# Dilated attention in a decoder trunk: whole causal score rows before, near blocks and the keys of the query's class modulo 4 after

## The reference

```python
DIL_PATTERNS = ((128, 1), (512, 4), (2048, 16))
def dilated_prompt(q, k, v):
    outs, lses = [], []
    for w, d in DIL_PATTERNS:       # the rows of each class modulo d, apart
        o, lse = band_attn(sub(q), sub(k), sub(v), w // d)   # 0 <= t - j <= w // d
        ...
    return combine_branches(outs, lses)
```

## Time and profile before

| | |
|---|---|
| runs | 2828.29, 2823.35, 2825.64 us; median 2825.64 |
| profiled execution | 2823.23 us, its span 2821.4 |
| TensorE, share of the span | 99% |
| DVE, POOL, ACT | 62%, 51%, 33% |
| granted TensorE clock, mean | 0.999 |
| dilated attention with its linear units, first score to the end of the last pair | 1460 to 1727 us of the span |

### The profile page before, as it was taken

How to read it: one execution, slowest core, us unless ns; L and a number is a source line. 1 busy time by engine, 2 the same in 40 slices (tenths; PEclk the granted TensorE clock), 3 DMA queues, 4 the chain that set the end, 5 groups by cost and what they waited for, 6 DMA issues and landing times. The chain is left out here.

```text
span 2821.4 us, 61139 instructions
## 1 busy us (share of the span) xinstructions
PE 2795.2 (99%) x22743; PEld 2661.7 (94%) x22743; DVE 1739.8 (62%) x3258; ACT 931.0 (33%) x2089; POOL 1450.0 (51%) x1178
## 2 busy tenths in 40 slices
PE   9999999999999999999999999999999999999998
PEld 8888999999999999999987778999999999999998
DVE  5555642248766676977953346523468666668877
ACT  4333422133322222433324445212324222224433
POOL 3222343332677777877431112433334777777775
PEclk9999999999999999999999999999999999999999
DMA  4111133421223232642222222234312232326432
GB/s 138 38 30 38 60 113 130 153 85 37 90 105 119 75 119 105 233 143 82 65 76 84 84 76 69 86 133 148 120 46 76 83 111 105 119 76 231 128 128 76
DMA packets 79799, 283.05 MB, mean 100 GB/s; under 512 B 10959, under 2 KB 16975, under 8 KB 70665
## 3 DMA queue, kind: packets, MB, share of 16 engines
q10 hardware_dynamic: 41581, 148.18, 14.7%
q1 hardware_dynamic: 38051, 132.55, 13.9%
HBM read 223.45 MB, written 57.49 MB: 100 GB/s over the span
## 5 line engine op out<-in xcount | busy, mean ns | idle before, releaser
L681 POOL TENSOR_SCALAR w_hi<-w_raw 128x512 fp32r<-128x512 f32 x236 | 153.1, 667 | 989.6 <-PE linear L830 779.3
L685 POOL TENSOR_TENSOR w_lo<-w_raw,w_hi 128x512 fp32r<-128x512 f32 x420 | 590.9, 1419 | 98.0 <-ACT w_hi L1654 82.6
L830 PE MATMUL linear<-h_hi,w_hi 128*128 128x344 f32 x1134 | 373.7, 330 | 1.2 <-issue 0.5
L830 PE MATMUL linear<-h_hi,w_lo 128*128 128x344 f32 x1134 | 362.2, 319 | 0.0
L830 PE MATMUL linear<-h_lo,w_hi 128*128 128x344 f32 x1134 | 362.2, 319 | 0.0
L685 POOL TENSOR_TENSOR w_lo<-w_sum,w_hi 128x512 fp32r<-128x512 f32 x186 | 268.8, 1445 | 147.1 <-ACT w_hi L1654 146.5
L1218 PE MATMUL ps_scores<-c,w_hi 128*128 128x258 f32 x1512 | 288.5, 283 | 0.0
L1218 PE MATMUL linear<-c,w_hi 128*128 128x258 f32 x1344 | 247.3, 284 | 1.3 <-POOL w_lo L685 1.3
L830 PE MATMUL linear<-g_hi,w_hi 128*128 128x344 f32 x744 | 240.2, 323 | 0.0
L830 PE MATMUL linear<-g_hi,w_lo 128*128 128x344 f32 x744 | 237.7, 320 | 0.0
L830 PE MATMUL linear<-g_lo,w_hi 128*128 128x344 f32 x744 | 237.4, 319 | 0.0
(11 more groups left out here) (478 smaller groups left out, 7302.1 us busy)
## 6 DMA issues: line engine op xcount, KB each, us to landing
w_raw<-in_w SPq DMA_DIRECT2D x214, 512.0 KB, 3.7
hid_spill<-hid_out ACTq DMA_DIRECT2D x22, 1032.0 KB, 4.4
t_spill<-hid_joined ACTq DMA_DIRECT2D x20, 1032.0 KB, 3.9
y_val<-t_spill ACTq DMA_DIRECT2D x40, 516.0 KB, 4.1
kv_slotc<-in_mem_cache_k ACTq DMA_DIRECT2D x8, 2048.0 KB, 8.5
kv_slotc<-in_mem_cache_v ACTq DMA_DIRECT2D x8, 2048.0 KB, 10.2
w_more<-in_w SPq DMA_DIRECT2D x32, 512.0 KB, 5.5
y_val<-hid_spill ACTq DMA_DIRECT2D x30, 516.0 KB, 3.9
```

The costliest lines, as they stand in the source:

```text
L681: pool.tensor_scalar(out, src, 1.0, 0.0, ALU.mult, ALU.add).then_inc(sem["hi_split"], 1)
L685: return pool.tensor_tensor(out, src, hi.bitcast(F32), ALU.subtract).then_inc(sem[event], 1)
L830: mm = pe.matmul(out, w[:, slot, cols], a, start=(k == 0 and j == 0), stop=(k == n - 1 and j == 2))
```

## The change

It takes the query blocks in rising order, one piece each. A piece holds the query's own and the preceding key block in full (near), and of all earlier blocks the keys of the query's class modulo 4 (far): 32 per block. Queries are taken by class: the 32 queries 4a + r are the weights of class r, and write the output partitions 32r to 32r + 31, once against far keys (every fourth, starting at r) and once against near keys. The far probabilities come first in a row, then the near. They are transposed by blocks of 128 columns; where the far width isn't a multiple of 128, the last block's surplus rows, which are near probabilities, are zeroed in ACT's copy by a factor from `rows1`. The far values have to lie by class: each pair's values go from `vnat1` to a DRAM scratch and back as `vfar1` (position 128 x class + feature, partition = key / 4). The near part of V is as before, the far part has a matmul per 128 far keys, class and head, with 32 columns. The mask is 448 wide and the same for all blocks.

```diff
-PIECES = [(qb, 4 * part, min(4, qb + 1 - 4 * part), part == 0, 4 * part + 4 > qb)
-          for qb in reversed(range(QB)) for part in range(1 + qb // 4)]
-SAMPLE_S = 8
+BLOCK_ORDER = (0, 1, 2, 3, 4, 5, 6, 7)
+CLASSES = 4
+FAR = P // CLASSES
+PIECES = [(qb, max(0, qb - 1), min(2, qb + 1), FAR * max(0, qb - 1)) for qb in BLOCK_ORDER]
+SAMPLE_S = 5
-HALVES = [2 if piece[2] > 2 else 1 for piece in PIECES] + [1]
+HALVES = [2 if piece[3] else 1 for piece in PIECES] + [1]
...
-LAST_FILL = [("S", 3), ("V", 0), ("T", 1), ("S", 4), ("V", 1), ("T", 2), ("S", 5), ("V", 2), ("T", 3), ("S", 6), ("V", 3), ("T", 4),
-             ("S", 7), ("V", 4), ("T", 5), ("S", "sample"), ("V", 5), ("T", 6), ("S", 8), ("V", 6), ("T", 7), ("S", 9), ("V", 7),
-             ("S", 10), ("T", 8), ("S", 11), ("V", 8), ("T", 9)]
+LAST_FILL = [("S", 3), ("V", 0), ("T", 1), ("S", 4), ("V", 1), ("T", 2), ("S", "sample"), ("V", 2), ("T", 3), ("S", 5), ("V", 3), ("T", 4),
+             ("S", 6), ("V", 4), ("T", 5), ("S", 7), ("V", 5), ("T", 6)]
+LAST_SPLITS = {3: (0,), 4: (1,), "sample": (2,), 5: (3, 4), 6: (5, 6), 7: (7, 8)}
+LAST_BEGINS = {"sample": (0,), 5: (1, 2), 6: (3, 4), 7: (5, 6)}
 DIL_WIDE = {1: [("S", 1)],
             2: [("S", 2), ("T", 0)],
-            3: [("S", 3), ("V", 0), ("T", 1)],
-            4: [("S", 4), ("V", 1), ("T", 2)],
...
-            11: [("S", 10), ("T", 8)],
-            12: [("S", 11), ("V", 8), ("T", 9)]}
+            4: [("S", 3), ("V", 0), ("T", 1)],
+            5: [("S", 4), ("V", 1), ("T", 2)],
+            7: [("S", "sample"), ("V", 2), ("T", 3)],
+            8: [("S", 5), ("V", 3), ("T", 4)],
+            10: [("S", 6), ("V", 4), ("T", 5)],
+            11: [("S", 7), ("V", 5), ("T", 6)]}
-DIL_DRAIN = {0: [("V", 9), ("T", 10)], 1: [("V", 10), ("T", 11)], 2: [("V", 11), ("T", "sample")], 3: [("V", "sample")],
-             4: [("R", "sample")]}
+DIL_DRAIN = {0: [("V", 6), ("T", 7)], 1: [("V", 7), ("T", "sample")], 2: [("V", "sample")], 3: [("R", "sample")]}
...
+        v_scratch = nc.dram_tensor("v_scratch", (SEQ, P), F32, kind="Internal").ap()
...
@@ TensorE, score @@
-                        for h in range(2):
-                            r = HEAD * h
-                            for c in range(0, P, 32):
-                                mm = pe.matmul(ps_s[c:c + 32, 512 * h:512 * h + P * nb],
-                                               q1_of[i][r:r + HEAD, P * qb + c:P * qb + c + 32],
-                                               keys1[i][r:r + HEAD, P * kb:P * kb + P * nb], start=True, stop=True)
+                        for of, start, end, step_ in (("far", 0, far * CLASSES, CLASSES), ("near", P * kb, P * kb + P * nb, 1)):
+                            for h in range(2):
+                                for r in range(CLASSES if end > start else 0):
+                                    rows, first = slice(HEAD * h, HEAD * h + HEAD), start + (r if of == "far" else 0)
+                                    to = 512 * h + (0 if of == "far" else far)
+                                    mm = pe.matmul(ps_s[FAR * r:FAR * r + FAR, to:to + (end - start) // step_],
+                                                   q1_of[i][rows, P * qb + r:P * qb + P:CLASSES], keys1[i][rows, first:end:step_],
+                                                   start=True, stop=True, skip_group_check=True)
...
@@ TensorE, mix (behind the near part) @@
+                    if far:
+                        pe.wait_ge(loads["vfar"], 16 * i + 16)
+                        pe.wait_ge(sem["turned_in"], at("turned_in", ph, 0, done + 2))
+                        for b in blocks_of(k, 1):
+                            for c in range(CLASSES):
+                                for h in range(2):
+                                    r, at_ = HEAD * h, place_in_half(h, 1, b) + FAR * c
+                                    mm = pe.matmul(ps_o[r:r + HEAD, FAR * c:FAR * c + FAR], vfar1[:, b, P * c + r:P * c + r + HEAD],
+                                                   pt1[:, at_:at_ + FAR], start=False, stop=(b == blocks_of(k, 1)[-1]),
+                                                   skip_group_check=True)
...
@@ ACT, exponential @@
-                    act.wait_ge(sem["biased"], at("biased", ph, 0, BIAS_ORDER.index(k if k == "sample" else closing(k)) + 1))
+                    act.wait_ge(sem["biased"], at("biased", ph, 0, BIAS_ORDER.index(k) + 1))
...
@@ ACT, step S, behind the exponential of the piece before @@
+                        if k == (4 if i == PAIRS - 1 else 1):
+                            act.wait_ge(values_out, 16 * i + 16)
+                            if i:
+                                act.wait_ge(sem["mixed"], at("mixed", ph))
+                            act.dma_start(vfar1[:, :, :], v_scratch.rearrange("(s j r) d -> j s (r d)", s=2, r=CLASSES)
+                                          ).then_inc(loads["vfar"], 16)
...
@@ ACT, step T @@
+                            if full:
+                                mm = copy(out[:, :, 0:full], in_[:, :, 0:full])
+                            if rest:
+                                mm = copy(out[:, :, full:w], in_[:, :, full:w], scale=rows1[:, rest // FAR - 1:rest // FAR])
...
@@ ACT, behind values_in @@
+                act.wait_ge(sem["v_ready"], at("v_ready", ph, 0, 1))
+                act.wait_ge(loads["vfar"], 16 * i)
+                act.dma_start(v_scratch.rearrange("(b p) d -> p b d", b=QB), vnat1[:, :, :]).then_inc(values_out, 16)
...
@@ DVE, scale (its output now in the order of the classes; the wait at the stage's start is on 48 instead of 32) @@
-                    dve.tensor_tensor(out, ps_o[:, 0:P], out, ALU.mult).then_inc(sem["scaled"], 1)
+                    out = mix1[:, 4 + i, P * qb:P * qb + P].rearrange("p (a r) -> p r a", r=CLASSES)
+                    dve.tensor_tensor(out, by_class(ps_o[:, 0:P]), out, ALU.mult).then_inc(sem["scaled"], 1)
```

More of the change, by code:

```diff
@@ L77, in blocks_of, with place_in_half, source_block @@
 def blocks_of(k, half):
[L79 to L88, removed]
+    return range(-(-PIECES[k][3] // P) if half else PIECES[k][2])
+def place_in_half(h, half, b):
+    return 512 * half + 256 * h + P * b
+def source_block(k, h, half, b):
+    return P1_WIDTH[k % 3] * h + (0 if half else PIECES[k][3]) + P * b
@@ L1540, in mix @@
                         return
-                    qb, kb, nb, opens, closes = PIECES[k]
+                    qb, kb, nb, far = PIECES[k]
                     if k == 0 and i == PAIRS - 1:
                         pe.wait_ge(sem["v_ready"], at("v_ready", ph, 0, 1))
[L1544 to L1550, removed]
-                            for h in range(2):
-                                r, at_ = HEAD * h, place_in_half(h, m)
-                                mm = pe.matmul(ps_o[r:r + HEAD, 0:P], vnat1[:, kb + m, r:r + HEAD], pt1[:, at_:at_ + P],
-                                               start=(opens and m == 0), stop=(closes and m == nb - 1), skip_group_check=True)
+                    pe.wait_ge(sem["scaled"], at("scaled", ph, 0, k))
@@ new lines, in mix @@
+                    pe.wait_ge(sem["turned_in"], at("turned_in", ph, 0, done + 1))
+                    for m in blocks_of(k, 0):
+                        for h in range(2):
+                            r, at_ = HEAD * h, place_in_half(h, 0, m)
+                            mm = pe.matmul(ps_o[r:r + HEAD, 0:P], vnat1[:, kb + m, r:r + HEAD], pt1[:, at_:at_ + P],
+                                           start=(m == 0), stop=(m == nb - 1 and not far), skip_group_check=True)
+                    mm.then_inc(sem["mixed"], 1)
@@ L1628, in _ @@
                         step(what, k)
-                        if what == "S" and k in range(5, 12):
-                            begin_out(k - 5)
+                        for n in LAST_BEGINS.get(k, ()) if what == "S" else ():
+                            begin_out(n)
                 if i + 1 in Q_AHEAD:
@@ L1635, in _ @@
                 last = step
-            for position in range(5):
+            for position in range(4):
                 drain(position)
@@ L2374, in step @@
                     past_waits()
[L2375 removed]
+                    for n in LAST_SPLITS.get(k, ()) if i == PAIRS - 1 and what == "S" else ():
                         act.wait_ge(sem["tile_done"], at("tile_done", ph, 0, 6))
[L2378 removed]
+                        high_piece(mix1, h_hi, *SOONER[n])
                     if what == "S":
@@ L3589, in masks @@
     new[:, 384] = 8.0 * np.log(3.0)
-    return table(window, 256), table(dilated, 1024), np.zeros((P, 129), np.float32), new
+    query = np.array([CLASSES * a + r for r in range(CLASSES) for a in range(FAR)])
+    near = P + query[:, None] - np.arange(2 * P)[None, :]
+    far = CLASSES * ((QB - 1) * FAR + query[:, None] // CLASSES - np.arange((QB - 2) * FAR)[None, :])
+    both = dilated(np.concatenate([far, near], axis=1)).astype(np.float32)
+    return table(window, 256), both, np.zeros((P, 129), np.float32), new
```

140 lines of the change are left out of this document (64 added, 76 removed).

## The result

The changed kernel takes 2789.57 us (median of four runs, 2787.07 to 2794.43); the kernel before, run in turn with it, took 2826.08 (four runs, 2823.35 to 2828.29). The ratio is 0.9873, 95% interval 0.9856 to 0.989: 1.3% faster, clear of no change. The forecast was 2789, the range 2778 to 2806.

What follows compares the result with a forecast made beforehand. TensorE was taken to bound the kernel, busy 99% of the span. Gains of 10.3 us per pair, 30.9 for three, plus 5.3 in the last, made 36.2: from the median of 2825.64 to 2789 us, range 2778 to 2806.

Steps and rivals of the forecast that it cites:

- V: Probabilities times values on TensorE: 9.7 us per pair before, 8.15 after (near 4.50, far 3.65), gain 1.5.
- What bounds the stage: TensorE bounds the dilated attention: busy for 70.30 of 71.69 us in the second pair, so only its work or waits count.
- the period: Time from one turning of values to the next: about 61 us forecast, against 71.69 before.
- T: Transposes on TensorE: 72 become 46 per pair, 2.73 us gained.
- the breaks: Switches between linear matmuls and attention steps, 0.17 us each: 17 become 13 per pair, 0.7 us gained.
- the stalls: TensorE's waits at the first T and at the end of the fill: 0.64 and 0.75 us gained per pair.
- Rival 1: In V's far part a short matmul costs as much as a long one: 3.2 us worse per pair, 2802; chance 0.2.
- S: Scores of one piece on TensorE: 9.68 us per pair before, 4.58 near plus 1.12 far after, gain 3.98.
- Rival 2: Strided operands are slow in S: twice the time for far columns gives 2793 us, four times 2802; chance 0.2.
- The last pair: Nothing there hides the trip of the values; it gains 5.3 us, a 2.4 us wait included.
- So it waits 2.4 us: In the last pair TensorE waits for the far values ahead of a far part of V, bounds 0 and 6.
- The trip: Values to DRAM and back, 4.6 us each way: costed at nothing where hidden, 11 us of cover in the second pair.

Runs made afterwards that it cites:

- e6: Changed kernel with the last S, V and T steps of the fill one position later in the first three pairs; 2793.42 us, one run.
- e4: Changed kernel with 8 moving columns instead of 32 in each far matmul of V; 2791.0 us, one run.
- e5: Changed kernel with 64 moving columns instead of 32 in each far matmul of V; 2791.3 us, one run.
- e8: Changed kernel without the trip of the values through DRAM, far values loaded once from other data; 2790.19 us, ratio 0.9876.
- e0: The changed kernel itself, unedited, measured again; 2791.7 us, ratio 0.9881 to the kernel before.
- e1: Changed kernel with far keys read as a contiguous run instead of every fourth column; 2786.29 us, ratio 0.9867 to the kernel before.
- e3: Changed kernel with the queries read as contiguous runs of 32 instead of every fourth; 2791.65 us, one run.
- e9: Changed kernel with keys and values kept by class within each block of 128 tokens, so far keys are contiguous; 2790.52 us, one run.

## Why the prediction was right

- **What bounds the stage** was right: with TensorE idle for next to nothing in the first three pairs, the time fell by what was taken from it and by nothing else. No idle time before T0, and none at T6 and T7 there, came as forecast; the period is 62.20 for about 61.
- **T, the breaks and the stalls** came within 0.15 us a pair: 3.62 for 3.48, 0.71 for 0.7. Both stalls of the earlier trace rows are gone, T0's wait (0.57) and that between position 12 and drain 0; e6 puts the latter back and pays 1.1 us. That T0's wait came from `closing` fits, but no run puts `closing` back.
- **V** was right in its mechanism and its price: 8.05 us for 8.15, V with one far block 1.03 for 1.05. Rival 1 fell: 0.54 us for eight passes where it had 0.86; e4 and e5 show that the moving columns don't set the pace, the rows with one moving column that the weight columns do. The near part alone came out 0.61 under its 4.50 and the far part 0.51 over its 3.65: a V step's fixed share, counted with the near part, lies by the starts at the end of the far part now (0.54 is 0.46 and 0.08). Of the 0.46 that V gained beyond the forecast, 0.3 lie in the sum of before, 10.01 us where single steps gave 9.7: V in drain 0 (from 1586.84) waited another 0.26 us for ACT's spread, at 1587.98, behind the rows shown in the earlier trace rows.
- **S** is the step that failed, in size. "I take the contiguous rate, that of the nearest rows", 5.70 us; it is 7.13. Rival 2 was right, at its lower price (twice), and the sentence that took the queries' weight loads to be covered was wrong by 0.32. I had its mechanism, its bounds and the rule, and chose against them on the ground that two clocks per column leave slack. At four elements apart they don't. The first three pairs so gained 28.4 us for 30.9 (9.44, 9.49, and 9.49 taken for the third): 4.3 less by S, 1.4 more by V, 0.4 more by T.
- **The last pair** made up for it: 6.06 in its own stretch and 2.3 in the third's, 8.3 for 5.3. "So it waits 2.4 us" failed: ACT reached the load 1.6 us sooner, the load took 0.7 less, and TensorE came 0.4 later. The idle time of the stretch grew by 0.2 us, not by 2.85. A wait did stand there, at another place (V1, behind the issues), but the earlier trace rows held 2.8 us of idle time already.
- **The trip costs nothing in three pairs**: shown by e8. In the last it costs 0.94 us, at a place that the prediction had not looked at: ACT "then owes a high piece" took that piece to start right behind the values, as in the earlier trace rows.
- The forecast of 2789 was met to 0.6 us by two misses of 2.5 and 3.0 that cancel. With S as measured in all four pairs and the rest as predicted it would have been 2795, still in the range.

The profiled spans differ by 29.0 us and the medians by 36.5; the stage alone gained 36.8. The first turning of values, ahead of which the kernels differ next to nothing, begins at 1451.80 us in the profile of before, 1456.63 in that of after, 1456.22 in e0, 1453.40 in e1 and 1455.77 in e3; behind the stage after takes another 2.9 us more than before. Unchanged code scatters by up to 5 us between profiles, which is why effects of 1 us were read from marks inside the stage. What in that code scatters was not looked into.

## What to carry to other kernels

Count the bytes between the elements that TensorE reads: in these scores a moving float32 operand with a stride of two ran at full rate, with a stride of four at half; a layout that is written with the stride once by an engine with time to spare gives it back (here 1.1 us of 62.2 a pair). Where a short matmul has few columns, price it by its weight load, not its columns. Where the work around a stretch runs out, ask of each DMA issue on a compute engine's queue whether it waits for that engine's own last result: then it is time in which the engine does nothing, and the wait is to be looked for in who stands behind it rather than in the transfer. When steps are moved, compare the whole stage and not one stretch of it.

## What was not expected

- A DMA issue on ACT's queue takes 0.34 to 0.60 us. Beside a running ACT instruction it cost nothing; two in a row behind a wait for ACT's own copy left it without work for 1.17 us. In the last pair this, not the transfer, was what the round trip of the values cost (0.94 us).
- Strided weights (32 columns at a stride of four) cost 0.03 to 0.05 us per S step, 0.32 a pair, where the prediction took them to be covered.
- Far parts of 32 and 64 contiguous keys take the same time to 0.01 us (0.75 in e1, 0.74 in e9): from 64 columns to 32 a pass of eight 64x32 tiles gets no shorter.
- DVE wrote the permuted layout (256 columns, stride of 128 bytes) in 0.62 us where 344 contiguous columns took 0.52: scattering is slower there, yet beside TensorE it cost only the 0.2 us ahead of the last turning.
